# A decoder step with expert gathers: all 128 dot products of the first tile inside the next projection, paced by the weight slots

## What is computed

```
h = rmsnorm(x); z = h @ w_in                     # 2048 x 6200
y = concat(short conv, attention with three branches, mLSTM)   # all from z
x = x + y @ w_out                                # 2048 x 2048
h = rmsnorm(x)
q = h @ wq;  s1, s2 = products of q with the sub-keys; top 16 of each, top 16 of the 256 sums
eidx = the 16 experts of each of 8 heads;  g = softmax(top)
act = gelu(sum_d h[t,d] * u[eidx])               # 128 dot products per row
x = x + sum_k (g * act) * v[eidx]                # 128 scaled rows per row
y = rmsnorm_final(x)
```

## Time and profile before

| | us |
|---|---|
| time, median of three runs | 3142.41 (3140.25 to 3149.76) |
| the profiled execution, its own time | 3155.58 |
| its span, first to last instruction | 3153.8 |
| VectorE busy | 2002.3 (63%) |
| TensorE products busy | 1620.9 (51%) |
| POOL busy | 1069.4 (34%) |
| ScalarE busy | 270.9 (9%) |
| DMA moved | 992.93 MB, mean 315 GB/s |

### The profile page before, as it was taken

One profiled execution on the slowest core, in us unless ns is written; L12 is line 12 of the kernel. 1 busy time (PEld: TensorE's weight loads), 2 busy tenths in 40 slices (PEclk: granted clock), 3 DMA queues, 4 the chain that ended last, 5 costly groups with the idle time before them and its releaser, 6 DMA issues.

```text
span 3153.8 us, 20040 instructions
## 1 busy us (share of the span) xinstructions
PE 1620.9 (51%) x6113; PEld 1014.0 (32%) x6113; DVE 2002.3 (63%) x2607; ACT 270.9 (9%) x590; POOL 1069.4 (34%) x644
## 2 busy tenths in 40 slices
PE   7985947777798756633676677225784000000000
PEld 3454642222235532623554565111384000000000
DVE  0024157777603864663777777686554899999998
ACT  1012110000001200100111112100000000000000
POOL 0000003222300222201333433223220688888885
PEclk9975978888997568766888788656755555555555
DMA  9942739999952659827999999758993799999997
GB/s 283 306 126 104 262 116 361 414 414 414 413 174 70 240 219 387 346 79 281 396 395 387 385 394 381 243 193 298 376 378 160 323 422 422 422 422 421 422 422 322
DMA packets 267342, 992.93 MB, mean 315 GB/s; under 512 B 31217, under 2 KB 60598, under 8 KB 183432
## 3 DMA queue, kind: packets, MB, share of 16 engines
q0 software_dynamic: 92160, 671.13, 52.3%
q1 hardware_dynamic: 174072, 319.40, 29.3%
q10 hardware_dynamic: 1040, 1.59, 0.1%
HBM read 980.73 MB, written 19.77 MB: 317 GB/s over the span
## 4 chain that ended last, share of the span: by engine, by line
PE 37%; DMA 23%; POOL 16%; DVE 14%; issue 5%; SPq 4%; ACT 2%; DVEq 0%; POOLq 0%; ACTq 0%
POOL arena L1584 16%; PE ps L724 12%; DMA arena<-in_w_in_dram 9%; PE ps L865 6%; DMA arena<-in_cache_nsa_kv_dram 5%; PE ps L843 4%; DMA arena<-in_w_out_dram 3%; PE ps L360 2%; DMA arena<-in_peer_wq_dram 2%; DVE arena L1072 2%; SPq L565 2%; SPq L566 2%; PE ps L363 2%; DVE arena L1150 1%; DMA arena<-in_peer_v_dram,arena 1%
## 5 line engine op out<-in xcount | busy, mean ns | idle before, releaser
L1584 POOL DMA_INDIRECT arena<-in_peer_u_dram,arena x320 | 458.1, 1432 | 1544.3 <-DVE arena L1069 803.6
L1069 DVE CUSTOM_DVE_ANT_0 arena<-arena 128x2048 bf16<-128x2048 f32 x320 | 733.2, 2291 | 199.8 <-DMA arena<-in_peer_u_dram,arena 197.3
L1584 POOL DMA_INDIRECT arena<-in_peer_v_dram,arena x320 | 611.1, 1910 | 510.1 <-DVE arena L1072 287.6
L1072 DVE SCALAR_TENSOR_TENSOR arena<-arena 128x2048 f32<-128x2048 f32 x296 | 695.9, 2351 | 109.9 <-DMA arena<-in_peer_v_dram,arena 68.0
L724 PE MATMUL ps<-arena 128*128 128x512 f32 (+1 forms) x1152 | 548.2, 632 | 93.5 <-DMA arena<-in_w_in_dram 91.5
L724 PEld LDWEIGHTS ps<-arena 128*128 128x128 f32 (+1 forms) x1152 | 203.5, 184 | 437.0 <-issue 320.0
L865 PE MATMUL ps<-arena 128*128 128x128 f32 (+1 forms) x1536 | 236.3, 333 | 37.6 <-DMA arena<-in_peer_wq_dram 37.6
L865 PEld LDWEIGHTS ps<-arena 128*128 128x128 f32 x1536 | 234.8, 248 | 39.0 <-DMA arena<-in_peer_wq_dram 27.6
L843 PE MATMUL ps<-arena 128*128 128x512 f32 (+1 forms) x384 | 192.0, 663 | 54.9 <-DMA arena<-in_w_out_dram 54.9
L1184 DVE COPY arena<-ps 64x256 f32<-64x256 f32 (+1 forms) x24 | 9.1, 377 | 291.5 <-PE ps L742 290.8
L360 PE MATMUL ps<-arena 128*128 128x128 f32 x512 | 77.4, 327 | 185.7 <-DMA arena<-in_cache_nsa_kv_dram 185.7
(11 more groups left out here) (326 smaller groups left out, 1604.6 us busy)
## 6 DMA issues: line engine op xcount, KB each, us to landing
arena<-in_w_in_dram SPq DMA_DIRECT2D x96, 1024.0 KB, 5.3
arena<-in_w_out_dram SPq DMA_DIRECT2D x48, 1024.0 KB, 10.6
arena<-in_peer_wq_dram SPq DMA_DIRECT2D x48, 1024.0 KB, 6.7
arena<-in_cache_nsa_kv_dram SPq DMA_DIRECT2D x128, 384.0 KB, 9.0
arena<-in_cache_nsa_kv_dram SPq DMA_DIRECT2D x128, 128.0 KB
arena<-in_state_win_kv_dram SPq DMA_DIRECT2D x32, 256.0 KB
out_s_win_dram<-in_state_win_kv_dram SPq DMA_DIRECT2D x1, 8064.0 KB
arena<-in_peer_u_dram,arena POOLq DMA_INDIRECT x320, 10.3
```

Source lines behind the costliest of these rows:

```text
L1069: nc.vector.tensor_tensor_reduce(out=PROD, in0=rows_in, in1=H[t], scale=1.0, scalar=0.0, op0=ALU.mult, op1=ALU.add, accum_out=DOTS[:, c:c ...
L1072: nc.vector.scalar_tensor_tensor(out=ACC[t], in0=rows_in, scalar=GG[:, t, c:c + 1], in1=ACC[t], op0=ALU.mult, op1=ALU.add).then_inc(g_used, 1)
L1584: nc.gpsimd.indirect_dma_start(BUF[SLOT[p]], None, tables[kind], bass.IndirectOffsetOnAxis(EIDX[:, t, c:c + 1].bitcast(U32), 0)).then_inc( ...
```

## The change

All 128 `u` takes of tile 0 lie in the projection of t = 1, and they are no longer one piece. For each of the 48 slots VectorE first waits until `w_used` has reached the slot's number less two, and then takes 2, 3 or 3 rows. `gates(0)` follows directly, in front of the `QT` copies; on ScalarE `gelu_exp(0)` moves in front of the gate exponential. The takes in the units are now `v` columns of tile 0. `V_MID` becomes 64 and 128: all `v` of tile 0 lie before the tail. The block of takes before tile 2's routing has 20 instead of 24, and the 12 takes of tile 0 in the tail go.

```
-V_MID = [48, 116]
+V_MID = [64, 128]
...
                     act.wait_ge(a_z, 13 * t + 17)
+                    if t:
+                        gelu_exp(0)
...
                         if n + 1 < NU:
                             unit_exp(n + 1)
-                    if t:
-                        gelu_exp(0)
...
                 if t == 1:
-                    take(112)
+                    for i in range(W_IN):
+                        dve.wait_ge(w_used, W0[1] + max(i - 2, 0))
+                        take(3 if i % 3 else 2)
+                    gates(0)
...
                         if t:
                             take(1)
-                    if t:
-                        gates(0)
...
                 if t:
-                    take((None, 20, 24)[t])
+                    take(20)
...
             take(COLS[2])
             gates(2)
-            take(COLS[0] - V_MID[1])
             dve.sem_inc(v_x2, 1)
```

## The result

The changed kernel takes 3094.6 us (median of four runs, 3087.3 to 3101.3) against 3146.1 us (four runs, the three of the table above and a fourth); the ratio is 0.9835, 95% interval 0.9803 to 0.9867. That is 51.5 us less. Forecast were 64 us less, 3078 us, with a range of 3060 to 3110. The profiled execution took 3101.3 us with a span of 3099.5, 54.3 us less than the profiled one of before.

A forecast was written before the change was run, and what follows sets the result against it. The projection was taken as DMA-bound until 862 us, then TensorE-bound with DMA 46% busy. Projection -29, gates 0, units 0, tile 2 -5 and tail -30 sum to -64: from the median 3142.4 to 3078 us, range 3060 to 3110.

The forecast's parts named there:

- The projection: Tile 1's input projection: DMA-bound throughout, ending at 947 us instead of 976, -29 us, bounds -44 and 0.
- I take the middle: Projection's end: 151 to 155 MiB after 541.2 us give 942 to 952 us; 947 was taken.
- The price of 2.566 us: DMA time per MiB, from 125 MiB of slots and gathers in 320.8 us of the earlier projection.
- slots every 9 to 10 us: Sign in the projection's new profile: weight slots at this spacing from about 600 us on.
- The starvation rival: Projection: gathers always outstanding, each slot 11.9 us, +71 us instead of -29, 3178 us in all; chance 0.06.
- The gates: Tile 0's gates: +3.1 us in front of the QT copies, -3.1 behind the units; net 0, bounds -2 and +3.
- The units: Attention units: 16 takes become v rows of equal cost while TensorE sets the pace; 0 us.
- tile 2: Block before tile 2's routing: four gathers fewer beside the peer_wq slots, one slot less starved; -5 us, bounds 0 and -10.
- the tail: End of the kernel: 12 of 268 gathers go at 2.47 us each; -30 us, bounds -28.6 and -30.8.
- no gaps in the stream: Denies the rival that holding starts gathers late, so the projection still ends at 976; 3107 us, chance 0.13.
- no lower clock: Denies the rival that short waits keep TensorE at 1.2 GHz, 14.6 us a slot, over 100 us more; chance 0.02.
- no tail unshortened: Denies the rival that the tail's takes overlap something else, so it does not shrink; 3108 us, chance 0.04.

The follow-up runs named there:

- lead0: The changed kernel with the hold two slots tighter: takes of slot i wait until i slots are used, not i - 2; 3089.6 us.
- lead6: The changed kernel with the hold four slots looser: takes of slot i wait for i - 6; 3115.6 us.
- hold_only: The kernel before with its 112 projection takes held by the weight slots, two slots behind, and nothing moved; 3090.2 us.
- move alone: The changed kernel without the hold: 128 takes in one piece at the start of the projection; 3138.6 us.
- the second hold: Takes before tile 2's routing also held by the second expert matrix's slots; beside the tighter first hold, 3081.8 us with the move, 3072.6 without.
- wq_hold: The changed kernel with the 20 takes before tile 2's routing also held by the second expert matrix's slots, one slot behind; 3086.9 us.

## Why the prediction was right, and where its sizes were off

**The projection: right mechanism, term too large.** Forecast 29 us off its end. Measured were 18.5 off its end (957.5, outside the 940 to 955 of the signs) and 19.9 off its length, since it began 1.4 us later. The term's parts from the profile: six slots 46.6 us (45.5 before), then 400.8 us to slot 48, then 13.0 to the end. The 13 is as forecast; the middle was put at 393. The mis-sized step is "I take the middle" of 151 and 155 MiB. The two rows from 543.70 to 944.50 moved 412 GB/s x 377.0 us + 397 x 23.8 = 164.8 MB, 157 MiB. The price of 2.566 us was taken per MiB counted, and in its stretch 414 GB/s x 320.8 us = 126.7 MiB moved for the 125 counted, so 155 counted are the same 157 moved. The upper count was the right one. At its price it gives 398 us; the other 3 are the lower rate, 411 GB/s against 414. So nothing was lost to gaps, and all gathers, the four of `v` fetched ahead among them, were issued in front of the last slot. POOL's timeline shows the first and last of those four, 20 and 6 us before slot 48 begins at 944.5:

```profile
924.49 0.94 POOL L1584 DMA_INDIRECT arena<-in_peer_v_dram,arena  x1 [0.30 <-issue]
...
938.41 0.94 POOL L1584 DMA_INDIRECT arena<-in_peer_v_dram,arena  x1 [0.30 <-issue]
```

lead0 and lead6 show that this is an effect of the lead: what is released late competes with less. In lead0 three of these four are issued behind the start of slot 48, from 938.3 us on, and DMA is busy 0.86 of the last 13 us instead of 0.19. In lead6 all four are out at 922.3 us, 41 us before slot 48. The sum also took the landing of slot 48 for the last wait. It was slot 45's (920.73): slots 46 to 48 had landed when TensorE came to them. In lead0 slot 48 is waited for again (0.65 us).

**The slots' form: wrong.** The sign "slots every 9 to 10 us" took a mean for a pattern. The starvation rival described half of it: while gathers are in flight, the weights come at 11.7 to 12.3 us a slot, held or not. The pause that the rival lacks comes as runs of two to five slots, not as a quarter of each. The Trainium skill (DMA: Bandwidth & Descriptors, Queues, rings and completion order) says that each DMA engine drains a whole packet of one queue row before it turns to the next row. With the mean packets of the earlier trace rows, 7.3 and 1.8 KB, in turn, the weights would get a fifth of the stream, an estimate of 2.566 / 0.20 = some 12.8 us a slot; the 11.7 to 12.3 us of the changed kernel agree. Whether the profile's packets are the page's, which hold several descriptors, no run here shows.

**The gates: right.** +3.3 in front (27.5 against 24.2) for +3.1; behind the units, from the first unit scores to the output-gate reciprocal (L1128), 96.2 us before and 93.3 after, -2.9 for -3.1.

**The units, tile 2 and the tail: right.** `peer_wq` -5.8 for -5 in the profiled pair, -5.3 to -5.4 in the other kernels with 20 unheld takes (119.7, 119.8). Tail -29.7 for -30, within 0.8 us in all seven other kernels with 256 gathers. For the 48 takes up to tile 1's routing no cost shows, but the last column of the table could hide one of several microseconds.

**Sum.** The stages explain -20.0 - 5.8 - 29.7 = -55.5 us and the rest +1.2, for the span's 54.3. Of the 10 us missing to 64, the projection has 9. Against the forecast of 3078 the median of 3094.6 is 16 us more: 12 because the medians differ by 51.5 and not by 64, and 4 because a fourth run raised the median of before from 3142.4 to 3146.1. The other rivals stayed out: no gaps in the stream, no lower clock through the projection (0.92 on average), no tail unshortened. One reading was wrong, and nothing rested on it: slice 12 of the earlier trace rows is not nearly idle but about half busy (174 GB/s); the lowest is slice 13, with 70.

**What the prediction did not ask.** It credited the change as one. The four corners say that hold alone gives 58.5 us, move alone 10 and both 51.5; the intervals of hold alone and both overlap. With the hold in place the move is worth nothing that these runs can tell from zero, because the stage that it fills and the stage that it empties are then both DMA-bound: 16 MiB more in the projection cost 34.4 us (426.0 to 460.4), the tail gives 29.9 back and `peer_wq` 6.3. With the second hold `peer_wq` takes 110 us either way, and the move costs: 449.0 + 664.1 us of projection and tail against 415.2 + 694.3, 3.6 us, while the medians stand 9 us apart (3081.8 against 3072.6). What makes up the other 5 us was not found, and the place of the gates and the rows in the units differ as well; the two profiled spans (3070.2 and 3070.8) do not show it.

## What to carry to other kernels

When two streams share a saturated DMA and one of them ends early, look for the stretch behind it in which the other's engine is alone: that idle DMA time is what can be gained, and a wait that paces the faster stream by the slower one's progress gains it without moving anything. Keep the lead of the paced stream as small as its latency allows; each slot of lead here cost TensorE's time less DMA's time for a slot. Moving transfers from one DMA-bound stage to another gained nothing here, though the tail that they left was 30 us shorter; test pace and place apart.

## What the runs showed of the hardware that was not expected

A held stream does not thin out evenly. With 2.67 gathers admitted per slot, TensorE still got its slots every 11.7 to 12.3 us while gathers flew, and worked through two to five slots at 7.2 us each between (up to seven in hold_only, with 2.33 admitted). The length of such a stage scatters: with the same code in this stage it took 460.4, 462.2 and 465.4 us in three kernels (the gates' place behind it differs in one). In tile 2's `peer_wq` stage of wq_hold, TensorE was granted its lower clock (0.50, 1.2 GHz) through 110 us of 128x64 products with no wait at all, after 0.88 from 2240 to 2249 us. So filling its waits does not bring the clock back there. Its weight loads were busy for 109 us of the 110 as well; why the clock stays low remains open.
